# Prompt attention at the loop's start, output weights split inside the loop, first group's norm in the drain: a hybrid attention and convolution layer on one core

## What is computed

```python
s = einsum('bqhmd,bkhmd->bhmqk', qblk, k) * HEAD_DIM ** -0.5
p = softmax(s, axis=-1)
att = einsum('bhqk,bkhe->bqhe', p[:, :, 0] - lam * p[:, :, 1], v)      # per query block

att  = rms(att, subln_w) * (1 - lam_init)                              # _finish
att  = att.reshape(b, n, D_ATT) * silu(g_att)
conv = cb * short_conv(cc * ch, conv_w, conv_b) * silu(g_conv)
y    = concatenate([att, conv], axis=-1) @ w_out
out  = x + gate * y
```

## Time and profile before

| | us |
|---|---|
| three runs | 1803.90, 1803.21, 1800.39 |
| median | 1803.21 |
| the profiled execution, its own time | 1802.25 |
| its span, first to last instruction | 1800.4 |
| TensorE busy in the span | 1685.2 (94%) |
| VectorE, ScalarE, GpSimd busy | 1044.2, 790.8, 755.0 |
| mean granted TensorE clock | 0.976 of 2.4 GHz |

### The profile page before, as it was taken

How to read it: one execution, slowest core, us unless ns; L and a number is a source line. 1 busy time by engine, 2 the same in 40 slices (tenths; PEclk the granted TensorE clock), 3 DMA queues, 4 the chain that set the end, 5 groups by cost and what they waited for, 6 DMA issues and landing times.

```text
span 1800.4 us, 25386 instructions
## 1 busy us (share of the span) xinstructions
PE 1685.2 (94%) x8526; PEld 1464.5 (81%) x8526; DVE 1044.2 (58%) x1393; ACT 790.8 (44%) x1659; POOL 755.0 (42%) x807
## 2 busy tenths in 40 slices
PE   3899999989999999999789999999999999679999
PEld 1688888879999999999668888888888888568889
DVE  2553887863242332422567777777777777365553
ACT  3562333330010100100478888888888888321110
POOL 0000888860000000000378888888888888200000
PEclk8899999999999999999999999999999999779999
DMA  9962223231020120111341041014111100454441
GB/s 353 290 206 91 101 89 113 96 121 59 31 82 21 42 76 31 63 57 43 109 88 36 29 100 42 29 47 92 32 35 52 60 29 13 155 187 176 164 151 46
DMA packets 132626, 163.69 MB, mean 91 GB/s; under 512 B 10592, under 2 KB 121184, under 8 KB 131680
## 3 DMA queue, kind: packets, MB, share of 16 engines
q1 hardware_dynamic: 127440, 158.61, 27.4%
q10 hardware_dynamic: 5136, 4.46, 0.7%
HBM read 112.95 MB, written 50.07 MB: 91 GB/s over the span
## 4 chain that ended last, share of the span: by engine, by line
PE 77%; DVE 9%; DMA 4%; issue 4%; SPq 3%; ACT 2%; ACTq 1%; POOL 1%; DVEq 0%; POOLq 0%
PE ps L709 40%; PE ps L860 11%; PE ps L939 10%; PE ps L849 9%; PE ps L841 4%; DVE stt L1531 3%; DVE e L1513 2%; PE ps L773 2%; DMA scr<-in_xtok 1%; DMA scr<-in_xT 1%; PE ps L922 1%; DMA worw<-in_w_out 1%; DVE stt L1564 1%; DVE crs L1598 1%; ACT e L1179 1%
## 5 line engine op out<-in xcount | busy, mean ns | idle before, releaser
L709 PE MATMUL ps<-hT,w 128*128 128x448 f32 (+1 forms) x3360 | 691.7, 365 | 7.3 <-DVE w L1285 7.3
L709 PEld LDWEIGHTS ps<-hT,w 128*128 128x128 f32 x3360 | 623.5, 188 | 68.9 <-issue 19.6
L1531 DVE TENSOR_REDUCE stt<-ps 128x1 f32<-128x1024 f32 x256 | 312.6, 1221 | 138.9 <-PE ps L860 136.8
L860 PE MATMUL ps<-kb,qb 128*128 (+1 forms) x1280 | 333.5, 391 | 36.0 <-ACT e L1179 23.1
L1179 ACT ACTIVATE e<-ps,stt 128x1024 f32<-128x1024 f32 x256 | 285.7, 1116 | 130.0 <-DVE stt L1531 129.9
L849 PE MATMUL ps<-at,vb 128*128 128x256 f32 x1088 | 272.8, 381 | 0.0
L860 PEld LDWEIGHTS ps<-kb,qb 128*128 128x128 f32 x1280 | 205.1, 192 | 75.9 <-issue 22.3
L665 POOL TENSOR_TENSOR stt<-stt,lamc 128x2 f32<-128x2 f32 x64 | 12.6, 196 | 567.8 <-DVE stt L1556 567.8
L849 PEld LDWEIGHTS ps<-at,vb 128*128 128x128 f32 x1088 | 204.3, 191 | 36.1 <-issue 0.2
L671 POOL TENSOR_TENSOR e<-e,stt 128x512 f32<-128x512 f32 (+1 forms) x192 | 218.8, 1140 | 5.0
L939 PE MATMUL ps<-mix,wo 128*128 128x448 f32 (+1 forms) x960 | 203.6, 371 | 7.8 <-DVE mix L1610 7.8
(11 more groups left out here) (120 smaller groups left out, 1377.1 us busy)
## 6 DMA issues: line engine op xcount, KB each, us to landing
raw<-in_w_in SPq DMA_DIRECT2D x32, 512.0 KB, 3.9
qb<-spill_q SPq DMA_DIRECT2D x256, 64.0 KB, 2.3
scr<-in_xtok SPq DMA_DIRECT2D x8, 1024.0 KB, 8.1
wad<-in_w_ada SPq DMA_DIRECT2D x4, 2048.0 KB, 17.1
scr<-in_xT SPq DMA_DIRECT2D x8, 1024.0 KB, 6.6
spill_k<-scr SPq DMA_DIRECT2D x32, 224.0 KB, 2.2
spill_q<-scr SPq DMA_DIRECT2D x32, 224.0 KB, 2.2
mix<-spill_cv SPq DMA_DIRECT2D x8, 896.0 KB, 10.2
```

Source lines behind the costliest of these rows:

```text
L709: mm = pe.matmul(out, slot_of(l, j), rhs_of(r, j), start=(i == 0 and j == 0), stop=(i == 2 and j == DJ - 1))
L860: mm = pe.matmul(out[:, c0 - k0:c1 - k0], qb[:, t, ver, m], keys, start=(ver == 0), stop=(ver == 1))
L1531: dve.tensor_reduce(stt[:, b, 0, 3 * m + c:3 * m + c + 1], ps[:, 2 * c:2 * c + 2, :].rearrange("p c n -> p (c n)"), AX.X, ALU.max, negate= ...
```

## The change

- `load_prompt` no longer loads the prompt's values, and is called in the last conv head after the query load of group 1, when all weights are split. The values have a load of their own (`load_prompt_v`) behind `load_v(0, 1)`.
- The prompt's scores go to banks 5 and 6 (before: 0 and 1) after step 0, its transposes to bank 7 after step 2, its product to bank 7 after step 3. Before step 4 TensorE waits for the copy of that product. On VectorE `prompt_maps` is cut into six pieces, set into steps 1 and 2 by the table `PROMPT_AT`; on ScalarE the exponential follows step 1, both copies and the store follow step 3.
- Output weights: block i is loaded in step i + 4, its high part made on ScalarE at the end of step i + 5, its low part on VectorE behind the second maximum of step i + 6. They stay in SBUF to the end. To make room, `at` loses an unused half and the epilogue's buffers are laid over the loop's.
- The first group's attention result is loaded in step 60. Its four squares and roots, the four column sums (banks 0 to 3) and the four norms are placed between the drain's steps. VectorE makes both parts of the normed values itself (`mine`). The four first halves come behind all column sums. A gate load has its own semaphore (`c_ga`), and squares, roots and reciprocals share four buffers `csr`.
- Instruction streams: ScalarE's and VectorE's first four iterations are now written out (before three and two).

The diff, cut to its core ("..." marks what is left out):

```diff
+WO0 = 5
...
+                        if tg == 1:
+                            sp.wait_ge(w_lo, CHUNKS)
+                            load_prompt()
...
             load_v(0, 0)
             load_v(0, 1)
+            load_prompt_v()
             store_conv(H - 1, TG)
             sp.wait_ge(stored, 32 + 32 * H * NG)
             sp.wait_ge(aux_stored, 16 * (1 + H + H * NG))
-            load_prompt()
...
-                    if it == 4 * (H - 1) and t == 0:
-                        load_wo(0)
-                        load_wo(1)
...
+                    if WO0 - 1 <= n < WO0 - 1 + DJ:
+                        load_wo(n - WO0 + 1)
+                    if n == NT - 4:
+                        load_att(0)
+
+            load_mix(0)
+            load_gates(0)
             sp.wait_ge(t_mm, 5 * NT)
+            load_x(0)
...
 # TensorE
             for it in range(2):
                 for t in range(4):
                     n = 4 * it + t
+                    if n == S_PV:
+                        pe.wait_ge(pr_a, 3)
                     step(it, t, tr=n >= S_TR, tr_last=n > S_TR, pv=n >= S_PV)
+                    if n == 0:
+                        prompt_scores()
+                    if n == 2:
+                        prompt_transposes()
+                    if n == 3:
+                        prompt_product()
...
+            step(ITS, 0, sc=False)
             for h in range(H):
                 csums(h, GROUPS[0][1])
-                out_half(0, h, 0)
+            step(ITS, 1, sc=False, tr=False)
+            for o in range(H):
+                out_half(0, o, 0)
+            step(ITS, 1, sc=False, tr_last=False, pv=False)
+            step(ITS, 2, sc=False, tr=False)
+            step(ITS, 3, sc=False, tr=False, tr_last=False)
...
 # ScalarE
+                    step(it, t, tr=n >= S_TR, tr_last=n > S_TR, out=n >= S_OUT and t % 2 == 0, scale=n >= 1)
+                    if n == 1:
+                        prompt_exp()
+                    if n == 3:
+                        prompt_hi()
+                        prompt_out()
...
+                    if WO0 <= n < WO0 + DJ:
+                        wo_hi(n - WO0)
...
+            step(ITS, 0, sc=False, after=True)      # squares of group 0 behind its first portion
+            for h in range(H):
+                root(0, h)
+            step(ITS, 1, sc=False, out=False, scale=False)
...
 # VectorE
+            PROMPT_AT = {(1, 0): prompt_max, (1, 1): prompt_shift, (1, 3): prompt_den,
+                         (2, 0): prompt_coef, (2, 1): prompt_scale, (2, 2): prompt_add}
...
+                    if p == 1 and isinstance(n, int) and WO0 < n <= WO0 + DJ:
+                        wo_lo(n - WO0 - 1)
...
+            step(ITS, 0, sc=False)
+            step(ITS, 1, sc=False, den=False, comb=False)
+            dve.wait_ge(a1_ready, NT)
+            dve.wait_ge(t_mm, 5 * (NT - 2))
+            norm(0, 0, mine=True)
+            norm(0, 1, mine=True)
+            step(ITS, 2, sc=False, den=False, comb=False)
+            norm(0, 2, mine=True)
+            norm(0, 3, mine=True)
```

More of the change, by code:

```diff
@@ L932, in out_half @@
                         pe.wait_ge(c_mix[tg % 2], 32 * (tg // 2 + 1))
-                    wait(pe, o_used, k - 3)
+                    if k < H:
+                        pe.wait_ge(c_std, k + 1)
+                    else:
+                        pe.wait_ge(o_used, k - 3)
                 elif o == 0:
                     pe.wait_ge(c_lo, H * (tg + 1))
-                js = range(H) if half else range(H, DJ)
+                part = (mixc, mixa)[half][tg % 2]
                 for i, (l, r) in enumerate(((0, 0), (0, 1), (1, 0))):
-                    for j in js:
-                        mm = pe.matmul(ps[:, k % 4, 0:n], wo[:, o, l, j], mix[:, tg % 2, r, j, 0:n],
-                                       start=(half == 0 and i == 0 and j == H),
+                    for j in range(H):
+                        mm = pe.matmul(ps[:, k % 4, 0:n], wo[:, o, l, j + H * (1 - half)], part[:, r, j, 0:n],
+                                       start=(half == 0 and i == 0 and j == 0),
                                        stop=(half == 1 and i == 2 and j == H - 1))
@@ L1190, in step @@
                         tr_act(n - S_TR, (t - S_TR) % 4, p)
+                    if after and p == 0:
+                        for h in range(H):
+                            square(0, h)
                 if sc:
@@ L1609, in mix_lo @@
                 dve.wait_ge(c_hi, k + 1)
-                dve.tensor_tensor(mix[:, tg % 2, 1, h, 0:n], cy[:, k % 2, 0:n], f32(mix[:, tg % 2, 0, h, 0:n]),
+                dve.tensor_tensor(mixa[tg % 2][:, 1, h, 0:n], cy[:, k % 2, 0:n], f32(mixa[tg % 2][:, 0, h, 0:n]),
                                   ALU.subtract).then_inc(c_lo, 1)
-            for h in range(H):
-                norm(0, h)
-            mix_lo(0, H - 1)
+            for it in range(4):
+                for t in range(4):
+                    n = 4 * it + t
+                    step(it, t, den=n >= 1, comb=n >= S_COMB, tr_last=n > S_TR)
+            with dve.Fori(4, ITS) as it:
+                for t in range(4):
+                    step(it, t)
+            step(ITS, 0, sc=False)
[7 more added lines that the diff above has]
+            norm(0, 3, mine=True)
             for tg in range(NG):
```

262 lines of the change are left out of this document (127 added, 135 removed).

## The result

| | before | after |
|---|---|---|
| median of the runs beside each other | 1802.44 us | 1780.57 us |
| ratio, 95% interval | | 0.988, 0.9864 to 0.9895 |
| the profiled execution, its own time | 1802.25 us | 1778.94 us |
| its span | 1800.4 us | 1776.8 us |

The change takes 21.9 us off the time, 1.2%. The predicted time was 1780.5.

A forecast was written before the change was run, and what follows sets the result against it. TensorE, busy 94% of the span, was taken as the bound, so only its gaps and own work could be sold; 8.4 + 4.3 - 35.4 = -22.7 us from 1803.21 gave 1780.5, range 1768 to 1793.

The forecast's parts named there:

- Part 1, loads moved: 24 prompt loads moved into the projections: 15.6 us of SyncE time hidden, cost 0; the 6.10 us stall at step 4 goes.
- Part 2, seam +8.4: Prompt attention in steps 0 to 4: its chain makes the loop's start 8.4 us longer, bounds +3 and +13.
- The sum behind the exponential: After step 1's last maximum, VectorE's sum waits for ScalarE's prompt exponential, with step 2 queued behind: +4.0 us.
- Part 3, splits +4.3: Output weights split in steps 5 to 13: ScalarE and GpSimd paths of 3.8 us each overlap; 4.3 us, bounds 0 and 10.
- GpSimd's lock: In steps 5 to 13, VectorE's two-input SBUF splits block GpSimd, which sets the pace: least step 9.51 to 10.73, 3.8 us.
- Part 4, drain -35.4: After the loop, the second halves start at 1567.4 instead of 1602.79: -35.4 us, bounds -38 and -27.
- second rival: In the drain, half-clock first halves delay step 63's transposes, their copy and two norms by 8 us: 1788.5; chance 0.13.
- Behind the drain: 194.5 us unchanged: From the start of the second halves to the kernel's end, the same 194.5 us as before.
- extras absorbed: Rival for seam and splits: the extra work falls into waits, seam +3, splits 0, time 1771; chance 0.13.
- Both ends of the lock: Rival: GpSimd and VectorE hold each other up at splits and prompt scaling; seam +11, splits +10, 1789; chance 0.07.
- Slower: Rival: extra work leaves the loop in its long step, 10.8 us, to the end; +26 on top, 1806; chance 0.04.
- not as said: Rival in the drain: first group's norm still starts behind the last attention store, only weights saved; about 1800; chance 0.03.

The follow-up runs named there:

- run a: The changed kernel run again unaltered, as footing for the other runs on the same chip; median 1778.58 us, ratio 0.9868 to the kernel before.

## Why the prediction was right

The total was right within the spread of executions: -22.7 us foreseen, -23.6 found in the profiled ones, range and sign held. That 1780.5 met the median of 1780.57 to 0.1 us is luck: medians of the same kernel were 1778.58 and 1780.09 in the two other runs. Its steps were less exact: the loop was put 3.6 us too long (12.7 for 9.1) and the drain 2.2 us too short (-35.4 for -33.2), with 0.5 us from the loop's start and the end, and these errors stand against each other.

- **Part 1, loads moved: right.** Gate store foreseen at 823.0, found at 823.13; conv store as before; TensorE's last projection matmuls 68.92 us before and 69.12 after. The stall at step 4 was indeed the DMA's: without the prompt's chain step 4 waits for no load.
- **Part 2, seam +8.4: right in kind, too large.** Step 4's scores moved from 913.48 to 919.07, +5.6 (step 4's factors by 6.2, as the scores themselves run at half clock; the loop's 9.1 are these and the 3.0 of part 3). Two terms were mis-sized. The score matmuls were taken at half clock from the drain (3.14), and in their new place took 1.90, so step 0's short wait swallowed them: the next scores start at 880.59 against 880.15, +0.4, not +1.9. And step 2's first maximum came 3.6 us late, not 7.2: VectorE was 0.1 late where I had put 3.2, as the maximum and the subtraction went into waits entirely. The sum behind the exponential cost 3.5 of its 4.0, and step 2's own operations 1.7 of their 1.9 (ScalarE's factors of step 3 ended at 915.77, 5.35 late, not 9.1). The handover was foreseen as 2.4 us from ScalarE's factors to step 4's scores and took 3.3, of which 1.0 is the product at half clock (2.07).
- **Part 3, splits +4.3: size nearly right, one of its two reasons wrong.** From step 4's factors to step 13's the trace has 91.37 us before and 95.66 after: +4.3. The next twelve steps give 1.3 back (123.08 to 121.79), all of it in the two intervals behind step 13's factors (9.78 and 9.60 for 10.75 and 9.90): an even split lengthens one interval and shortens the next, which here lies behind the last split. Net +3.0, or four pairs with odd splits at 0.93 and 0.60 in turn, 3.06. I had named GpSimd's lock as a second path that costs as much. It stretches GpSimd as foreseen (10.73 for the least interval, found 10.51), but with the lock taken away the pair keeps its 21.36 us. The step that failed is reading "idle only 0.50 us in the shortest step" as "sets the pace": it has 1.7 in the long one, and a ring of two steps is set by their sum. Even and odd splits, with the rows behind an odd one, show ScalarE's reason right.
- **Part 4, drain -35.4: right.** Found -33.2 in the profile after and -34.9 in run a. With the start of step 63's factors as zero I had 34.3 us to the second halves; run a took 34.78, and VectorE's idle time ahead of the copy was 3.51 where I had 3.6. The 1.7 us more of the profile after are the half clock behind TensorE's wait for the last evacuation, which I had not in the sum. That is the second rival's mechanism, a delay on TensorE that the copy of step 63's transposes hands to VectorE, in a small size: 1.7 us instead of 8, since the first halves themselves ran at full clock (48 in 10.08).
- **Behind the drain: 194.5 us unchanged** was short by 0.7 us, all of it in TensorE's unbroken work from the second halves on (194.46 us before, 195.14 after); why is open.

Of the rivals, "extras absorbed" was half true, for the seam's first part. "Both ends of the lock" fell with the low parts left out; VectorE held up by GpSimd showed only where the sum was put later. "Slower" fell in the trace: the four intervals around steps 16 to 20 are 10.82, 9.53, 10.76 and 9.94, 41.05 us where before has 41.03. The ring keeps no memory of its extra work. For "not as said" nothing speaks: there is no weight DMA in the chain. That the weights are most of the drain's gain is not shown, since the prompt's attention left the drain with them.

## What to carry to other kernels

Work added to a pipelined loop costs what it adds to the ring's period, so look in which step of the period the engine idles: the same eight splits cost nothing in even steps and 0.6 to 0.9 us each in odd ones. A small chain that crosses engines costs far more than its matmuls (11.4 us for 3.6 here), and about half of that can hang on one handover; put each of its links into the middle of a step, ahead of work that is not late, and put the wait at the first instruction that truly needs it (6 us here for two lines). Test an engine that seems to set the pace by taking its excess away: its idle time in one step says little when the next one has more. And look at the granted clock behind each gap before a difference of 1 or 2 us is called an effect: two executions of one kernel differed by as much.

## What the runs showed of the hardware that was not expected

- A VectorE multiply of 8 columns with both inputs in SBUF took 0.17 us in the profile after, beside GpSimd's multiply of two columns, and 1.04 beside a GpSimd multiply of 512 columns, which took 1.04 us itself; a 512-column sum took 2.02 (1.52 in the profile after). The length of the small operation says nothing of what it can cost.
- The same gap of 1.72 us on TensorE was followed by full clock in one execution and by half clock in another of the same kernel (8 products in 1.89 and 3.48 us), and with that the drain came in two lengths, 34.8 and 36.4 us. Behind the prompt's transposes, after a gap of 2.33 us, the same happened in two kernels that are alike there: 4 score matmuls took 1.17 us in one and 2.06 in the other.
- A weight block that was issued behind eight loads of the next head landed 11.3 us after its issue, against 3.5 to 3.7 for the seven others of that kernel.
